# Two-block layer kernel: first three experts in a row, modulation parts between projections, second output weights in halves

## What is computed

```
def expert_block(args):
    xb, e = args
    hid = jax.nn.silu(xb @ w_gate[e]) * (xb @ w_up[e])
    return hid @ w_down[e]
```

## Time and profile before

| | |
|---|---|
| median of three runs | 1426.21 us |
| the profiled execution | 1425.91 us, its span 1424.2 us |
| TensorE busy (matmul) | 1294.1 us, 91% of the span |
| DVE, ACT, POOL busy | 39%, 25%, 11% |
| DMA | 303.87 MB, mean 213 GB/s; 299.23 MB read from HBM |
| expert weights, gate and up | 64 DMAs of 2048 KB, median 33.7 us to landing |
| expert weights, down | 32 DMAs of 2048 KB, median 36.8 us to landing |
| output weights (both) | 8 DMAs of 1024 KB, median 10.8 us to landing |
| chain of waits | TensorE 68%, DMA 20%, DVE 6%, ACT 3% of the span |

### The profile page before, as it was taken

The page is one execution under the profiler, slowest core; times in us unless marked ns, Lnnn a source line. Parts: engine busy times, 40 slices in busy tenths (PEclk is TensorE's granted clock), DMA queues, the critical chain, the costliest instruction groups (busy, mean ns, idle before and its releaser), DMA issues.

```text
span 1424.2 us, 21057 instructions
## 1 busy us (share of the span) xinstructions
PE 1294.1 (91%) x7518; PEld 640.9 (45%) x7519; DVE 558.8 (39%) x1041; ACT 356.6 (25%) x783; POOL 158.3 (11%) x276
## 2 busy tenths in 40 slices
PE   5989999999999999999999994899889788898786
PEld 2445656568944444644455453333333222333222
DVE  1466363745123333278787335222122111222124
ACT  1223232322145442212568220011011010111112
POOL 4011110202020000000000001211111111111110
PEclk9999999999999999999999995799999999999999
DMA  9151706142181110042213544389999999999994
GB/s 365 74 208 16 291 2 224 75 147 78 32 282 60 45 30 1 0 156 72 60 45 109 213 210 199 139 323 386 420 418 415 408 402 421 418 397 408 409 379 200
DMA packets 40048, 303.87 MB, mean 213 GB/s; under 512 B 7852, under 2 KB 8004, under 8 KB 22560
## 3 DMA queue, kind: packets, MB, share of 16 engines
q1 hardware_dynamic: 31520, 285.12, 50.9%
q0 software_dynamic: 8448, 17.67, 4.0%
HBM read 299.23 MB, written 13.75 MB: 220 GB/s over the span
## 4 chain that ended last, share of the span: by engine, by line
PE 68%; DMA 20%; DVE 6%; ACT 3%; issue 2%; POOL 1%; SPq 0%; DVEq 0%; ACTq 0%; POOLq 0%
PE bank L837 20%; DMA arena<-in_w_down 14%; PE bank L2795 9%; PE bank L768 8%; PE bank L2811 6%; PE bank L883 4%; DMA arena<-in_w_gu 3%; PE bank L946 2%; PE bank L826 2%; PE bank L2785 1%; DMA arena<-in_ada_w 1%; PE bank L1163 1%; PE bank L1107 1%; DMA arena<-in_w_out 1%; PE bank L1084 1%
## 5 line engine op out<-in xcount | busy, mean ns | idle before, releaser
L837 PE MATMUL bank<-hT,arena 128*128 128x512 f32 x720 | 318.3, 597 | 0.0
L2795 PE MATMUL bank<-arena,hT 128*64 128x512 f32 x1024 | 232.1, 602 | 25.0 <-DMA arena<-in_w_gu 23.5
L837 PEld LDWEIGHTS bank<-hT,arena 128*128 128x128 f32 x720 | 134.7, 190 | 161.2 <-issue 157.5
L2795 PEld LDWEIGHTS bank<-arena,hT 128*64 128x64 f32 x1024 | 72.2, 138 | 163.2 <-issue 135.6
L2811 PE MATMUL bank<-arena,yT 128*64 128x512 f32 x512 | 128.4, 648 | 17.7 <-DMA arena<-in_w_down 17.7
L768 PE MATMUL bank<-arena,yT 128*128 128x512 f32 x256 | 117.7, 615 | 5.7 <-DMA arena<-in_w_out 3.5
L2955 DVE TENSOR_SCALAR hT<-hT 128x256 f32<-128x256 f32 x32 | 9.4, 294 | 246.5 <-ACT hT L2906 239.4
L768 PEld LDWEIGHTS bank<-arena,yT 128*128 128x128 f32 x256 | 49.3, 197 | 66.1 <-issue 58.0
L2811 PEld LDWEIGHTS bank<-arena,yT 128*64 128x64 f32 x512 | 36.5, 147 | 85.4 <-issue 64.4
L2906 ACT ACTIVATE hT<-bank 128x256 f32<-128x256 f32 x32 | 12.3, 383 | 245.1 <-PE bank L2795 245.1
L883 PEld LDWEIGHTS bank<-arena 64*64 64x64 f32 x1856 | 59.3, 135 | 23.8 <-issue 14.4
(11 more groups left out here) (478 smaller groups left out, 1607.0 us busy)
## 6 DMA issues: line engine op xcount, KB each, us to landing
arena<-in_w_gu SPq DMA_DIRECT2D x64, 2048.0 KB, 33.7
arena<-in_w_down SPq DMA_DIRECT2D x32, 2048.0 KB, 36.8
arena<-in_w_in SPq DMA_DIRECT2D x53, 512.0 KB, 4.7
arena<-in_ada_w SPq DMA_DIRECT2D x24, 1024.0 KB, 5.0
arena<-in_w_ada SPq DMA_DIRECT2D x8, 1024.0 KB, 9.4
arena<-in_w_out SPq DMA_DIRECT2D x8, 1024.0 KB, 10.8
arena<-in_w_ada SPq DMA_DIRECT2D x8, 512.0 KB, 5.7
arena<-expert_rows SPq DMA_DIRECT2D x4, 1024.0 KB, 8.5
```

The costliest lines, as they stand in the source:

```text
L837: last = T.matmul(bank[0:rows, :], w[:, k, 0:rows], hT[:, k, :], start=k == 0, stop=k == KD - 1)
L2795: last = T.matmul(banks[1 + ub][MT * h:MT * h + MT, :], tile.xT[:, k, :], wgu[u][:, k // 4, :, k % 4, 256 * h:256 * h + 256], start=k == 0 ...
```

## The change

It touches three places.

1. Slices 0 to 2 of modulation group 1 are multiplied ahead of projection `("proj", 0, 3)`, slices 3 to 7 behind it. The wait on `s_first_in` moves along.
2. In `m1` the fox buffers come first, conv after them. `w_out_at` gives the second output weights' slices 4 to 7 the first 4096 columns and 0 to 3 the next. SyncE issues the two loads of slices 4 to 7 when fox's last product (`("fO", 7)`) is done, with `s_small`, and the other two after `s_m1free`. `first_tile` waits for the first two at its start and for the others ahead of slices 0 and 1.
3. The first three experts get programs of their own on TensorE (`first_experts`), ACT, DVE and POOL; overflow tiles of all three follow the three. The next round (experts 3 to 5) is written out, and the loop has eight rounds. Expert e of the first three uses slot (e + 2) mod 3, so that expert 3 (slot 0) takes the place of expert 1, expert 4 that of expert 2, and expert 5 that of expert 0; the places in `arena` of experts 0 to 2 are the same. SyncE waits for the expert that had the slot (`p`), and for overflow tiles only if that expert has some (`r_kept`, two small DVE operations). POOL's semaphores `xf` are given before TensorE's `rank` product; POOL gathers experts 0, 1 and 2 before the overflow tile's first gather. Three of the router's arrays move from `hT[:, 0..2]` to `hT[:, 5..7]`, since expert 0's rows are scaled into the first of those; the product with `last_hot` goes behind expert 0's gate-up.

```diff
         chunk_no = {name: n for n, name in enumerate(chunk_fill)}
...
+                for k in pairs:
+                    sp.dma_start(w_outs[i][:, w_out_at(i, k):w_out_at(i, k) + 2, :], v[:, k:k + 2, :]).then_inc(signal, 16)
 
             load_ada(KD)
             for n, name in enumerate(chunk_fill):
...
-            load_w_out(1, w_out2_v)
+            load_w_out(1, w_out2_v, s_wo, (0, 2))
             assert ada_sent[0] == len(ada_loads)
 
         ada_after = {("proj", 0, 3): KD + 1, ("proj", 1, 3): KD, ("proj", 2, 3): KD, ("proj", 3, 3): KD - 1}
@@ -765,7 +768,7 @@
         def pe_out_part(i, t, half, bank, ks, first, last):
 
...
             pe_proj(("proj", 0, 2))
             key_norm(0)
+            eng.wait_ge(s_first_in, 1)
+            for k in range(3):
+                pe_ada(1, k)
             pe_proj(("proj", 0, 3))
-            eng.wait_ge(s_first_in, 1)
-            for k in range(KD):
+            for k in range(3, KD):
                 pe_ada(1, k)
             bonus(0)
             for p in range(PAIRS):
...
         m1 = Arena()
-        un = m1.take(2, 542)
-        cv = m1.take(2, SEQ)
         fq = m1.take(2, SEQ)
         fk = m1.take(2, SEQ)
         fv = m1.take(TT, 256)
         cumk = m1.take(4, SEQ)
+        assert m1.at >= 4 * DM
+        un = m1.take(2, 542)
+        cv = m1.take(2, SEQ)
...
@@ -2148,20 +2154,23 @@
             def first_tile():
                 two = [fill(("out", 1, 0, half), 2 + half) for half in range(2)]
                 eng.wait_ge(s_m1free, 1)
+                eng.wait_ge(s_small, 80)
                 pe_out_part(1, 0, 0, two[0], (4, 5, 6, 7), True, False)
                 eng.wait_ge(s_ysq, 2)
                 both(("snorm", 0), (bsq[:, 0, :], bsq[:, 1, :]))
                 pe_out_part(1, 0, 1, two[1], (4, 5, 6, 7), True, False)
                 eng.wait_ge(s_ysq, 4)
                 both(("snorm", 1), (xdt[:, 2, :], xdt[:, 3, :]))
+                eng.wait_ge(s_wo, 64 + 32)
                 eng.wait_ge(s_y2, 1)
                 for half in range(2):
                     pe_out_part(1, 0, half, two[half], (0, 1), False, False)
                 eng.wait_ge(s_y2, 2)
                 for half in range(2):
                     pe_out_part(1, 0, half, two[half], (2, 3), False, True)
-            eng.wait_ge(s_wo, 128)
             pe_out(1, lambda t: None, first_tile, logits)
+            for tile in (*tiles, extra):
+                eng.sem_inc(tile.xf, 1)
 
             eng.wait_ge(s_chosen, 1)
             bank = fill(("rank",))
@@ -2424,11 +2433,12 @@
         STEPS = SEQ // MT - 1
         thr = tiny(STEPS)
         half_row = tiny()
-        r_half = hT[:, 2, 0:TT * MT].rearrange("p (n m) -> p n m", m=MT)
+        r_half = hT[:, 7, 0:TT * MT].rearrange("p (n m) -> p n m", m=MT)
         r_place = hT[:, 3, 0:NE + NOV]
```

The experts, cut to the waits and the orders:

```diff
-        r_half = hT[:, 2, 0:TT * MT].rearrange("p (n m) -> p n m", m=MT)
+        r_half = hT[:, 7, 0:TT * MT].rearrange("p (n m) -> p n m", m=MT)
...
+        r_kept = hT[0:1, 3, 64:64 + NE - 3]
...
-        hot_pos = hT[:, 0, :].rearrange("p (n m) -> p n m", m=MT)
-        hot_tile = hT[:, 1, 0:8 * (NE + NOV)].rearrange("p (n m) -> p n m", m=NE + NOV)
+        hot_pos = hT[:, 6, :].rearrange("p (n m) -> p n m", m=MT)
+        hot_tile = hT[:, 5, 0:8 * (NE + NOV)].rearrange("p (n m) -> p n m", m=NE + NOV)
...
-        ov_first = sb("ov_first", [1, NE + 1], i32)
+        ov_first = sb("ov_first", [1, 2 * NE - 2], i32)
+        KEPT_AT = NE + 1
...
+            dve.done(V.scalar_tensor_tensor(r_kept, r_nov[0:1, 0:NE - 3], 0.0, r_incl[0:1, 0:NE - 3], ALU.is_gt, MUL))
+            V.tensor_copy(ov_first[:, KEPT_AT:KEPT_AT + NE - 3], r_kept)
...
-        slot_w = [arena[:, 12288 * at:12288 * (at + 1)] for at in (1, 2, 0)]
+        slot_w = [arena[:, 12288 * at:12288 * (at + 1)] for at in (2, 0, 1)]
+        first_slot = lambda e: (e + U - 1) % U
...
-                body(0, u, u)
+                body(1, u, U + u)
...
-            with eng.Fori(1, ROUNDS) as it:
+            with eng.Fori(2, ROUNDS) as it:
...
+            def slot_before(e):
+
+                p = (1, 2, 0)[e - U] if isinstance(e, int) and e < 2 * U else e - U
+                at = KEPT_AT + p
+                src = ov_first[0:1, at:at + 1] if isinstance(e, int) else ov_first[0:1, bass.ds(at, 1)]
+                return p, eng.value_load(src, min_val=0, max_val=NOV)
...
-                n = extras_before(e - 2)
-                eng.wait_ge(first.gate_up, e - 1)
+                p, n = slot_before(e)
+                eng.wait_ge(first.gate_up, p + 2)
                 stand_alone(eng)
                 eng.wait_ge(more_.gate_up, n + 1)
                 stand_alone(eng)
...
-                    n = extras_before(e - 2)
-                    eng.wait_ge(first.down, e - 1)
+                    p, n = slot_before(e)
+                    eng.wait_ge(first.down, p + 2)
...
-            for u in range(U):
-                eng.wait_ge(s_slots, 2 if u < 2 else 3)
-                load_gate_up(u, u)
-                load_down(u, u)
+            for e in range(U):
+                eng.wait_ge(s_slots, 2 if e < 2 else 3)
+                load_gate_up(first_slot(e), e)
+                load_down(first_slot(e), e)
             eng.wait_ge(s_routed, 1)
             next_gate_up(0, U)
-            later_experts(eng, body)
+            experts(eng, body)
...
-                if not (isinstance(e, int) and e == 0):
-                    it0, u0 = before(it, u)
-                    scatter(tiles[u0], first, u0, e - 1, s_placed_col[0], e - 1)
+                it0, u0 = before(it, u)
+                scatter(tiles[u0], first, u0, e - 1, s_placed_col[0], e - 1)
                 if last:
                     extras(eng, e, more)
-            for u in range(2):
+            for u in range(U):
                 eng.wait_ge(tiles[u].xf, 1)
                 gather(tiles[u], u, u, s_picked[0], u)
...
+            for u in range(2):
+                eng.wait_ge(tiles[u].xf, 2)
+                gather(tiles[u], u, U + u, s_picked[0], U + u)
+            for e in range(U - 1):
+                scatter(tiles[e], first, e, e, s_placed_col[0], e)
+            for e in range(U):
+                extras(eng, e, more)
             experts(eng, body)
...
+            def turn_rows(tile, steps, n, turn, bank=0, bank_free=False):
+
+                if not bank_free:
+                    eng.wait_ge(steps.xT, n + 1)
...
+            def turn_last_hot():
+
+                eng.wait_ge(s_routed, 3)
+                for t in range(TT):
+                    for q in range(2):
+                        turned = T.matmul(banks[6][MT * q:MT * q + MT, CH(t)], last_hot[:, t, :], ident[:, :], start=True, stop=True)
+                turned.then_inc(s_spread, 1)
+
+            def first_experts():
+
+                def down_first(e):
+                    eng.wait_ge(w_dn[first_slot(e)], 16)
+                    down(tiles[e], first, first_slot(e), e, e)
+                turn_rows(tiles[0], first, 0, 0)
+                turn_rows(tiles[1], first, 1, 0, 7, True)
+                gate_up(tiles[0], first, first_slot(0), 0, 0, 0)
+                turn_last_hot()
+                turn_rows(tiles[2], first, 2, 0)
+                gate_up(tiles[1], first, first_slot(1), 1, 1, 0)
+                turn_rows(extra, more_, 0, 0, 7)
+                turn_hidden(tiles[0], first, 0)
+                gate_up(tiles[2], first, first_slot(2), 2, 2, 0)
+                down_first(0)
+                turn_hidden(tiles[1], first, 1)
+                turn_rows(tiles[0], first, U, 1)
+                eng.wait_ge(s_copied, 1)
+                down_first(1)
+                turn_hidden(tiles[2], first, 2)
+                down_first(2)
+                for e in range(U):
+                    overflow(0, first_slot(e), e, (e + 1) % U)
+
             def finish(it, u, e):
 
                 eng.wait_ge(w_dn[u], (it + 1) * 16)
                 down(tiles[u], first, u, e)
...
-                begun = isinstance(e, int) and e == 0
+                begun = isinstance(e, int) and e == U
...
-                if begun:
-                    turn_rows(extra, more_, 0, 0, 5)
...
-            eng.wait_ge(s_routed, 3)
-            for t in range(TT):
-                for q in range(2):
-                    turned = T.matmul(banks[6][MT * q:MT * q + MT, CH(t)], last_hot[:, t, :], ident[:, :], start=True, stop=True)
-            turned.then_inc(s_spread, 1)
-            turn_rows(tiles[0], first, 0, 0)
+            first_experts()
             experts(eng, body)
...
+            gate_exp(tiles[0], first, 0, 0)
             eng.wait_ge(s_spread, 1)
             for half, at in enumerate((yflat, hflat)):
                 last = S.activation(at[:, 3840:4096], banks[6][:, 256 * half:256 * half + 256], ACT.Copy)
             last.then_inc(s_copied, 1)
+            gate_exp(tiles[1], first, 1, 1)
+            hidden_out(tiles[0], first, 0)
+            gate_exp(tiles[2], first, 2, 2)
```

(22 more changed lines are left out.)

32 lines of the change are left out of this document (14 added, 18 removed).

## The result

Before: 1426.2 us (median of 4 runs); after: 1413.2 (1410.8 to 1414.5, 4 runs); ratio 0.9907, 95% interval 0.9895 to 0.9919. The change makes the kernel 13 us faster. The profiled execution of after is the slowest of its four: span 1412.8, 1414.5 with what lies around it. Set against that of before (1424.2), it is 11.4 us shorter.

The account below looks back on a forecast made before the run. From 933 us the expert weight stream at 404 GB/s was taken to bound the kernel, before that a serial program led by TensorE; 2.5 + 5.2 + 6.4 = 14.1 us off 1425.91 gave a predicted median of 1412.1, range 1407 to 1418.5.

Parts of the forecast that it names:

- the forecast case: Whole kernel: the three gains come through and the time falls within 1409 to 1415 us; chance 0.58.
- Part 1: Modulation parts, 67 to 87 us: load waits shrink, operands turned at 84.0 instead of 86.53; gain 2.5 us.
- Part 2: Second output weights, 782 to 793 us: 3.47 us idle TensorE and 1.8 us of low clock go; gain 5.2 us.
- Part 3: First experts: experts 0 to 2 in a row let weight loads go out sooner; stream's lead 6.4 us.
- the second hole: DMA stream ahead of expert 6's load: idle for 2.8 us, until 958.3 in before's time axis.
- first hole: DMA stream ahead of expert 5's load: idle for 2.7 us, from 937.2 to 939.9 in before's time axis.
- With 9.5 us it lands at 940, inside the wait for the hidden rows: Gather for the overflow's next tile, sent near 930: its landing at 940 falls within TensorE's 2.30 us wait.
- (a): Rival, first experts: late overflow makes holes of 11 us or more, the row gives almost nothing; 1417 to 1419; chance 0.14.
- (b): Rival, first experts: no holes, expert 5's load finds backlog, lead 11.9 us; 1406 to 1408; chance 0.11.
- (c): Rival, 67 and 783 us: early gains eaten by ACT and DVE, clock stays low; 1415.5 us; chance 0.10.
- (d): Rival, POOL's in-order queue: scatters delay expert 5's gather, DMA engines run dry, slower, 1431 with 25 us holes; chance 0.04.
- about 7 us at that rate: First experts: worth of the third part if the stream ran at 358 GB/s, 13% longer in both kernels.

Follow-up runs that it names:

- run 1: Moved modulation parts alone, on the kernel before; its trace has 2.3 us of gain, the interval of its runs is -2.9 to +0.6 us.
- run 11: Changed kernel with expert 2's output product computed twice, ahead of the overflow loop; 1413.7 us, ratio 0.9913.
- run 9: run 8 with expert 4's second weights loaded ahead of expert 5's first ones; 1407.1 us, ratio 0.9874.
- run 5: Changed kernel with expert 0's overflow loop ahead of the scatters of experts 0 and 1 in GpSimd's queue; 1413.6 us, ratio 0.9908.
- run 10: Changed kernel with only expert 4's second weights loaded ahead of expert 5's first ones; 1414.7 us, ratio 0.9925.
- run 8: Changed kernel with early overflow loop and expert 5 gather, expert 6's load in halves, counts read ahead, one branch around experts 1 and 2; 1409.6 us, ratio 0.9890.
- run 12: Changed kernel with expert 4's output product computed twice; 1413.3 us, ratio 0.9906.
- run 7: Changed kernel with expert 6's load in two steps, the first when half of expert 3's products are done; 1409.9 us, ratio 0.9896.
- run 4: Changed kernel with the semaphore for the first gathers put back behind the router's last product; 1416.5 us, ratio 0.9934.

## Why the prediction was right, point by point

**The whole.** 1412.1 predicted, 1413.2 measured, inside the 1409 to 1415 of the forecast case. Sum 14.1, measured 13.0. Some luck is in how close the profiled execution comes: it was 1.1 us late at part 1, won 1.5 at block 1's output products and lost 1.7 behind the stream, none of which was in a term.

**Part 1.** 2.5 predicted, 2.2 and 2.3 in two traces. One wait for part 7 of 1.17 us (1.3 predicted). Right in its place; run 1 doesn't resolve it in the time of the whole.

**Part 2.** 5.2 predicted, no idle time, 3.70 us for the products, 5.1 measured alone. Right.

**Part 3.** 6.4 predicted, 5.2 in the trace, 5.8 alone. The TensorE steps, shifted by the 7.9 us from before's axis: gate-ups end at 892.3, 901.3 and 909.8 in the prediction, 892.3, 901.2 and 909.6 in the trace; the three output products at 913.4, 918.5 and 923.2 against 913.1, 918.1 and 922.6. SyncE's loads: 901.4 against 901.49; 930.3 against 929.60; but 948.7 against 950.78 for expert 6, and there the second hole is 5.4 us where 2.8 were forecast; the first is 1.4 where it was 2.7. (By the prediction's own numbers, 911.0 plus 26 us is 937.0, so its first hole should have been 2.9 and its lead 6.2.)

The term that was mis-sized is the second hole, and the steps in it are two. "With 9.5 us it lands at 940, inside the wait for the hidden rows": it was issued at 922.75 and landed 8.1 us later, at 930.83, but TensorE turns those rows ahead of the hidden ones, and VectorE scales them ahead of making the hidden ones. A late gather does not lie inside that wait; it is added in front of it, 1.46 us, and the 2.29 us follow. And the 2.52 us behind the loop were in no term; the traces set side by side at run 11 tie them to the end of a packet of instructions. Bytes went at 410 to 422 GB/s in between, not at 404, so that the queue was empty sooner, which makes a hole longer without costing anything. Against them stood 0.7 us won on the gate-up before and 0.8 on the product of 5.37 us (6.17 taken).

**Rivals.** (a), gather under load and low clock, had a part of the mechanism of the miss, at a quarter of its size (1.5 us more of holes, where it wanted 5.5). (b) is what run 9 comes near, by other edits. (c) didn't happen (its own terms add up to 1415.2, not 1415.5). (d) was closer than its 0.04: the gather for expert 5 was issued at 952.31, landed at 961.36, and TensorE turned those rows at 961.45; in runs 5 and 11, where TensorE came 2.8 and 1.7 us sooner and the rows landed some 5.8 and 3.8 us later, it waited 8.7 and 5.6 us for them. The queue costs nothing in the changed kernel by a margin of nothing.

## What to carry to other kernels

Where a byte stream sets the end, ask which load closes the last hole and what frees its slot. An earlier load ahead of it moves holes about (run 10), unless the last hole is nearly closed (from run 8 to run 9). Work behind it costs nothing (run 12). Its own earlier release shortens the hole in the trace (run 7), though the gain in time was within the noise there and clear of it only with the other edits (run 9). Don't add up an engine's products up to that point: look also for waits that other work would fill, and for gaps that belong to something else, here very likely a packet of instructions (run 11). A semaphore given late on a busy engine's queue can be worth as much as the reordering it belongs to (run 4).

## What was not expected of the hardware

**A gap with no releaser, and instruction loading.** TensorE's idle time behind the overflow loop was 2.52 us here and between nothing and 2.37 in the kernels of the other runs. In after, one packet of the instruction queue ran just then, in the DMA view of 940.8 to 941.8 us (packets, MB, share of 16 engines' time):
```profile
q8 instruction: 1, 0.02, 5.8%
```
and the product followed at 943.47, 1.7 us after its end. The same distance stands in all ten traces of the table at run 11 in which such a packet ends near the product. In run 11 it ran in the view of 928.1 to 929.1 us instead, and none ran from there to 943.7:
```profile
q8 instruction: 1, 0.02, 5.5%
```
There the gap was 0.1 us. So the load of code very likely sets this gap. No run moved the packet alone, and the row doesn't say which engine's code it is; for TensorE's speaks only the constant distance. The Trainium skill (Advanced Engine Details and Errata, ISA Cache) gives 16 KB as the size of one line of instructions. The traces agree: the 55 packets of this queue in after carry 0.90 MB, some 16 KB each.

**Gathers beside a stream.** Gathers of 64 rows of 4 KB landed 3.9 us after the issue at 874.66, ahead of the stream, 8.1 us after it at 922.75, beside the stream, and 11.1 us after it for expert 5 in run 5. The Trainium skill (DMA: Bandwidth & Descriptors, Anatomy of one DMA) puts a transfer issued by GpSimd at about 2.0 us and its bytes at 436 GB/s, which makes 2.6 us for these (an estimate from that page). The gathers of after, 36 of them by source line, took:
```profile
DMA to landing us min/median/max: 3.1/9.4/12.9
```
The first six, ahead of the stream, took 3.1 to 3.9 us, near the estimate; the thirty beside the stream took 8.1 to 12.9, a factor of three and more.

**The rate.** A stretch without gathers ran at 430 GB/s (run 10, 927 to 933 us), the whole stream at 403 with them (953 to 1380 us). The Trainium skill (DMA: Bandwidth & Descriptors, Where 436 GB/s comes from) puts the limit at about 358 GB/s, which both exceed. The prediction's estimate that part 3 would be worth about 7 us at that rate only scales its 6.4; its own account redone at 358 GB/s, again an estimate, closes the first hole and all but 0.4 us of the second and gives some 10 us.
